# Gate and up of three feed-forward blocks by Strassen's scheme, four rounds of up and down, modulation dots on VectorE

## The reference, cut to what matters

```python
def swiglu(h, w1, w3, w2):
    return (jax.nn.silu(h @ w1) * (h @ w3)) @ w2

def _half_ffn(h, g, m, k, w1, w3, w2):
    y = swiglu(_modulate(h, g, m, k), w1, w3, w2)
    return h + (0.5 * m[:, :, 3 * k + 2] * y).astype(h.dtype)
```

## Time and profile before

| | |
|---|---|
| median of 3 runs | 2884.31 us (2883.98 to 2885.66) |
| span of the profiled execution (first to last instruction) | 2881.4 us |
| PE busy | 2789.6 us, 97% |
| DVE (VectorE) busy | 1520.7 us, 53% |
| ACT (ScalarE) busy | 1126.3 us, 39% |
| POOL (GpSimd) busy | 546.4 us, 19% |
| DMA | 258.76 MB, mean 90 GB/s |

### The profile page before, as it was taken

One profiled execution on the slowest core, in us unless ns is written; L12 is line 12 of the kernel. 1 busy time (PEld: TensorE's weight loads), 2 busy tenths in 40 slices (PEclk: granted clock), 3 DMA queues, 4 the chain that ended last, 5 costly groups with the idle time before them and its releaser, 6 DMA issues.

```text
span 2881.4 us, 40758 instructions
## 1 busy us (share of the span) xinstructions
PE 2789.6 (97%) x15696; PEld 2604.4 (90%) x15696; DVE 1520.7 (53%) x1919; ACT 1126.3 (39%) x1620; POOL 546.4 (19%) x264
## 2 busy tenths in 40 slices
PE   5999999999998999999999999999999999899999
PEld 5899999999986799999999999999998875788887
DVE  6974266564558668652664632222247657543332
ACT  3333134335547635331343422123324876532231
POOL 2442044210002522430442100000011520100000
PEclk8999999999999999999999999999999999999999
DMA  7443144212130014441442122212222110123232
GB/s 295 139 153 133 49 151 155 92 47 65 53 73 1 1 52 139 160 155 50 152 158 88 47 65 68 70 51 66 65 67 73 52 59 8 59 88 104 93 97 99
DMA packets 68391, 258.76 MB, mean 90 GB/s; under 512 B 7504, under 2 KB 9424, under 8 KB 67792
## 3 DMA queue, kind: packets, MB, share of 16 engines
q1 hardware_dynamic: 50736, 192.59, 20.3%
q10 hardware_dynamic: 17568, 65.02, 6.6%
HBM read 255.48 MB, written 2.10 MB: 89 GB/s over the span
## 4 chain that ended last, share of the span: by engine, by line
PE 86%; DVE 7%; issue 2%; ACT 2%; POOL 0%; DVEq 0%; POOLq 0%; ACTq 0%
PE banks L459 21%; PE banks L463 21%; PE banks L461 21%; PE banks L466 5%; PE banks L470 5%; PE banks L468 5%; DVE banks L1661 2%; PE banks L950 1%; PE banks L789 1%; DVE wl L1656 1%; PE banks L973 1%; DVE tmp L1849 1%; DVE xl L1841 1%; PE banks L873 1%; DVE nsS L2008 0%
## 5 line engine op out<-in xcount | busy, mean ns | idle before, releaser
L1079 ACT ACTIVATE wh<-raw 128x1024 fp32r<-128x1024 f32 (+1 forms) x300 | 338.8, 1129 | 1454.3 <-PE banks L463 1151.3
L459 PE MATMUL banks<-xh,wh 128*128 128x384 f32 x2608 | 671.6, 338 | 27.9 <-DVE wl L1656 15.8
L461 PE MATMUL banks<-xl,wh 128*128 128x384 f32 x2608 | 664.7, 335 | 0.0
L463 PE MATMUL banks<-xh,wl 128*128 128x384 f32 x2608 | 664.4, 335 | 0.0
L1656 DVE TENSOR_TENSOR wl<-raw,wh 128x1024 fp32r<-128x1024 f32 (+1 forms) x300 | 428.3, 1428 | 350.6 <-ACT wh L1079 349.8
L459 PEld LDWEIGHTS banks<-xh,wh 128*128 128x128 f32 x2608 | 471.7, 189 | 37.1 <-DVE wl L1656 19.0
L461 PEld LDWEIGHTS banks<-xl,wh 128*128 128x128 f32 x2608 | 473.9, 189 | 0.0
L463 PEld LDWEIGHTS banks<-xh,wl 128*128 128x128 f32 x2608 | 473.1, 189 | 0.0
L2419 POOL TENSOR_TENSOR mraw<-mraw,scb 128x1024 f32<-128x1024 f32 x120 | 316.1, 2635 | 636.2 <-DVE banks L1661 636.2
L463 PE MATMUL banks<-hh,wl 128*128 128x384 f32 x1056 | 267.9, 334 | 0.0
L461 PE MATMUL banks<-hl,wh 128*128 128x384 f32 x1056 | 267.9, 334 | 0.0
(11 more groups left out here) (368 smaller groups left out, 3240.4 us busy)
## 6 DMA issues: line engine op xcount, KB each, us to landing
raw<-in_w SPq DMA_DIRECT2D x176, 512.0 KB, 3.6
mraw<-in_wmn ACTq DMA_DIRECT2D x120, 512.0 KB, 4.4
raw<-in_w SPq DMA_DIRECT2D x64, 704.0 KB, 4.0
raw<-in_abin SPq DMA_DIRECT2D x24, 512.0 KB, 3.6
raw<-in_cdin SPq DMA_DIRECT2D x20, 512.0 KB, 3.6
mini<-in_wmn SPq DMA_DIRECT2D x9, 512.0 KB, 14.8
gmini<-in_wmn SPq DMA_DIRECT2D x2, 2048.0 KB, 21.8
raw<-in_about SPq DMA_DIRECT2D x8, 512.0 KB, 3.5
```

The source lines that it names most:

```text
L459: pe.matmul(bank(h), W, tokens(rh, h), start=(k == 0), stop=False)
L461: pe.matmul(bank(h), W, tokens(rl, h), start=False, stop=False)
L463: mm = pe.matmul(bank(h), L, tokens(rh, h), start=False, stop=(k == nk - 1))
L1079: act.activation(wh[slot][:, 0:nk * P], raw[slot][:, 0:nk * P], ACT.Copy).then_inc(hi_done, 1)
```

## The change

The gate and up products of ffn0, ffn1 and ffn2 are made in another way for chunks 4 to 21. Gate and up weights of a chunk, each cut in two at the middle of the 1024 inputs, are a 2x2 block matrix: A11, A12 (gate), A21, A22 (up). The activations are B11, B12 (inputs 0 to 511, even and odd blocks of tokens) and B21, B22. The Winograd form of Strassen's scheme is used:

- weight sums S1 = A21+A22, S2 = S1-A11, S4 = A12-S2 on VectorE (`weight_sum`), S3 = A11-A21 on GpSimd; each of S1, A11, S2, A22, S3, S4, A12 (128x512) is split in high and low part (`weight_hi` on ScalarE, `weight_lo` on VectorE);
- activation sums T1 = B12-B11, T2 = B22-T1, T3 = B22-B12, T4 = B21-T2, made once a block (`sums`, `sums_lo`, `first_sum_lo`) during its first group; T1 takes the place of B12 in `xh` and `xl`;
- seven products of 4 blocks x 3 matmuls x 384 columns in the order P1 = A11 B11, P5 = S1 T1, P6 = S2 T2, P7 = S3 T3, P3 = S4 B22, P2 = A12 B21, P4 = A22 T4;
- combinations u2 = P1+P6, uv = u2+P5, u2 = u2+P7, up's odd half = uv+P7, gate's odd half = uv+P3, up's even half = u2+P4 on VectorE, gate's even half = P2+P1 with a copy on ScalarE and the sum on GpSimd. Silu, the product and the split of the hidden chunk are then done by halves of 384 columns.

A block of ffn0 to ffn2 is now four rounds of up and down, of 4, 6, 6 and 6 chunks (the first with plain pairs), ffn3 three of 7, 7 and 8, all plain. The loops are written out. A modulation tile now gets both its dots on VectorE (`dot_mod`), none of the work on GpSimd or ScalarE. `mod_places` puts one tile beside each of the chunks 4 to 21, two beside chunks 2 and 3, and one beside each down tile of the second and third rounds (two beside two of them in ffn0, none beside two in ffn2), and 6 beside the last product of the ab mixer. The second half of the first gate's columns is loaded later, and its dots lie beside chunks 0 and 1. The other edits (semaphores that are merged, one transfer for the recurrence's weights) move nothing else.

```diff
-FH = FC // 2
+GROUPS = ((4, 6, 6, 6),) * 3 + ((7, 7, 8),)
+W_ORDER = ("S1", "A11", "S2", "A22", "S3", "S4", "A12")
+COMB_ORDER = ("U2", "U3", "C22", "C12", "C21")
...
+            def load_after_seven(t, s, src, nk):
+                slot = t % 2
+                sp.wait_ge(w_lo, w_count(s, "S3" if slot else "A12"))
                 sp.dma_start(raw[slot][:, 0:nk * P], src).then_inc(raw_landed[slot], 16)
...
+                            s = seven_pair(f, g, i)
+                            load_after_seven(t0 + 2 * i + 1, s - 1, src[1], KC)
+                            load_after_seven(t0 + 2 * i, s - 1, src[0], KC)
...
+            def seven_products(f, g, i):
+                pe.wait_ge(w_lo, w_count(s, "A11"))
+                pe.wait_ge(psum_free[1], t // 2 - 1)
+                product(P1_BANK[i % 2], "A11", *tokens(0, 0)).then_inc(p_done, 1)
+                pe.wait_ge(psum_free[0], t // 2)
+                product(P5_BANK, "S1", *tokens(0, 1)).then_inc(p_done, 1)
+                pe.wait_ge(w_lo, w_count(s, "S2"))
+                product(P6_BANK, "S2", *sums(0)).then_inc(p_done, 1)
+                if s:
+                    pe.wait_ge(comb_set, comb_count(s - 1, "C21"))
+                pe.wait_ge(w_lo, w_count(s, "S3"))
+                product(P7_BANK, "S3", *sums(1)).then_inc(p_done, 1)
+                pe.wait_ge(w_lo, w_count(s, "S4"))
+                pe.wait_ge(psum_free[1], t // 2)
+                product(P3_BANK, "S4", *tokens(4, 1)).then_inc(p_done, 1)
+                pe.wait_ge(w_lo, w_count(s, "A12"))
+                pe.wait_ge(half_set, 3 * s + 1)
+                product(P1_BANK[i % 2], "A12", *tokens(4, 0)).then_inc(mm_done, 1)
+                pe.wait_ge(comb_set, comb_count(s, "C22"))
+                product(P7_BANK, "A22", *sums(2)).then_inc(mm_done, 1)
...
+            def seven_act(f, g, i):
+                weight_hi(f, g, i, "A22")
+                weight_hi(f, g, i, "S3")
+                if i:
+                    hidden_hi(f, g, i - 1, 0)
+                act.wait_ge(p_done, 5 * s + 1)
+                act.activation(p1[:], P1_BANK[i % 2], ACT.Copy).then_inc(half_set, 1)
+                weight_hi(f, g, i, "S4")
+                weight_hi(f, g, i, "A12")
+                next_mods(f, ("up", first_chunk(f, g) + i))
+                if not last:
+                    weight_hi(f, g, i + 1, "S1")
+                act.wait_ge(comb_set, comb_count(s, "C12"))
+                act.activation(half(g1s[:], 1), half(g1s[:], 1), ACT.Silu).then_inc(half_set, 1)
...
+                    weight_hi(f, g, i + 1, "A11")
+                act.wait_ge(mm_done, t + 1)
+                act.activation(half(g1s[:], 0), thirds(P1_BANK[i % 2]), ACT.Copy).then_inc(psum_free[1], 1)
+                if not last:
+                    weight_hi(f, g, i + 1, "S2")
+                hidden_hi(f, g, i, 1)
+                act.wait_ge(pool_set, 2 * s + 2)
+                act.activation(half(g1s[:], 0), half(g1s[:], 0), ACT.Silu).then_inc(half_set, 1)
...
+            def last_quarter(f, g, i):
+                dve.wait_ge(mm_done, t + 2)
+                dve.tensor_tensor(half(hf[:], 0), thirds(u2), thirds(P7_BANK), ALU.add).then_inc(comb_set, 1)
+                dve.wait_ge(comb_set, comb_count(s, "C21"))
+                dve.wait_ge(half_set, 3 * s + 3)
+                dve.tensor_tensor(half(hf[:], 0), half(g1s[:], 0), half(hf[:], 0), ALU.mult).then_inc(hf_set, 1)
+
+            def seven_dve(f, g, i):
+                if i:
+                    last_quarter(f, g, i - 1)
+                weight_lo(f, g, i, "A22")
+                weight_lo(f, g, i, "S3")
+                if i:
+                    hidden_lo(f, g, i - 1, 0)
+                weight_lo(f, g, i, "S4")
+                dot_mods(f, ("up", first_chunk(f, g) + i))
+                if not last:
+                    weight_sum(f, g, i + 1, "S1")
+                dve.wait_ge(half_set, 3 * s + 1)
+                dve.wait_ge(p_done, 5 * s + 3)
+                dve.tensor_tensor(u2, p1[:], P6_BANK, ALU.add).then_inc(comb_set, 1)
+                dve.wait_ge(comb_set, comb_count(s, "U2"))
+                dve.tensor_tensor(uv, u2, P5_BANK, ALU.add).then_inc(psum_free[0], 1)
+                weight_lo(f, g, i, "A12")
+                if not last:
+                    weight_lo(f, g, i + 1, "S1")
+                dve.wait_ge(p_done, 5 * s + 4)
+                dve.tensor_tensor(u2, u2, P7_BANK, ALU.add).then_inc(comb_set, 1)
+                dve.wait_ge(psum_free[0], t // 2 + 1)
+                dve.tensor_tensor(half(hf[:], 1), thirds(uv), thirds(P7_BANK), ALU.add).then_inc(comb_set, 1)
+                dve.wait_ge(p_done, 5 * s + 5)
+                dve.tensor_tensor(half(g1s[:], 1), thirds(uv), thirds(P3_BANK), ALU.add).then_inc(comb_set, 1)
+                if last:
+                    split_lo(t + 2, 0, n)
+                else:
+                    weight_sum(f, g, i + 1, "S2")
+                    weight_lo(f, g, i + 1, "A11")
+                    weight_sum(f, g, i + 1, "S4")
+                dve.wait_ge(half_set, 3 * s + 2)
+                dve.wait_ge(comb_set, comb_count(s, "C22"))
+                dve.tensor_tensor(half(hf[:], 1), half(g1s[:], 1), half(hf[:], 1), ALU.mult).then_inc(hf_set, 1)
+                if not last:
+                    weight_lo(f, g, i + 1, "S2")
+                hidden_lo(f, g, i, 1)
...
-            def prod_mods(it0):
+            def seven_pool(f):
+                        for q in range(2):
+                            pool.wait_ge(raw_landed[q], 16 * (t // 2) + 16)
+                        if s:
+                            pool.wait_ge(w_lo, w_count(s - 1, "S3"))
+                        pool.tensor_tensor(W_SRC["S3"], W_SRC["A11"], W_SRC["A21"], ALU.subtract).then_inc(pool_set, 1)
+                        pool.wait_ge(psum_free[1], t // 2 + 1)
+                        pool.wait_ge(half_set, 3 * s + 1)
+                        pool.tensor_tensor(half(g1s[:], 0), half(g1s[:], 0), thirds(p1[:]), ALU.add).then_inc(pool_set, 1)
```

More of the change, by code:

```diff
@@ L65, with first_chunk, up_tile, down_tile @@
 N_TILES = _t
+def first_chunk(f, g):
+    return sum(GROUPS[f][:g])
+def up_tile(f, g):
+    return BASE[f"ffn{f}"] + 2 * first_chunk(f, g) + KC * g
+def down_tile(f, g):
+    return up_tile(f, g) + 2 * GROUPS[f][g]
+def seven(f, g):
+    return f < 3 and g > 0
+NSEVEN = FC - GROUPS[0][0]
+def seven_pair(f, g, i):
+    return NSEVEN * f + first_chunk(f, g) - GROUPS[f][0] + i
+_seven = [False] * N_TILES
+for _f in range(4):
+    for _g in range(len(GROUPS[_f])):
+        if seven(_f, _g):
+            for _q in range(2 * GROUPS[_f][_g]):
+                _seven[up_tile(_f, _g) + _q] = True
+PLAIN = [0]
+for _v in _seven:
+    PLAIN.append(PLAIN[-1] + (not _v))
+W_ORDER = ("S1", "A11", "S2", "A22", "S3", "S4", "A12")
+def w_count(s, name):
+    return 7 * s + W_ORDER.index(name) + 1
+COMB_ORDER = ("U2", "U3", "C22", "C12", "C21")
+def comb_count(s, name):
+    return 5 * s + COMB_ORDER.index(name) + 1
+def sum_count(s, name):
+    return 3 * s + ("S1", "S2", "S4").index(name) + 1
+def mod_places():
+    where = []
+    for f in range(3):
+        place = {}
+        for ch in (2, 3):
+            place["up", ch] = 2
+        for ch in range(4, FC):
+            place["up", ch] = 1
+        for g in (1, 2):
+            for j in range(KC):
+                place["down", g, j] = 1
+        if f == 0:
+            place["down", 1, 2] = place["down", 2, 2] = 2
+        if f == 2:
+            place["down", 2, 2] = place["down", 2, 5] = 0
+        where.append(place)
+    m, out = 0, []
+    for f in range(3):
+        start = m
+        table = {}
+        for g, n in enumerate(GROUPS[f]):
+            for key in [("up", first_chunk(f, g) + i) for i in range(n)] + [("down", g, j) for j in range(KC)]:
+                table[key] = range(m, m + where[f].get(key, 0))
+                m += where[f].get(key, 0)
+        out.append((start, m, table))
+        if f == 0:
+            m += AB_MODS
+    assert m == 120, m
+    return out
+W2_ROW = {}
+_rows = {}
+for _f in range(4):
+    for _g, _n in enumerate(GROUPS[_f]):
+        W2_ROW[_f, _g] = _rows.get(_n, 0)
+        _rows[_n] = W2_ROW[_f, _g] + 1
+AB_MODS = 6
+MODS = mod_places()
+AB_MOD0 = MODS[0][1]
 PCOL = {}
@@ new lines, in dot_mod, with dot_mods @@
+            def dot_mod(m, vec, vec_n, bufs):
+                dve.wait_ge(mod_landed[m % 2], 16 * (m // 2) + 16)
+                dve.wait_ge(scb_ready, vec_n + 1)
+                for q in range(2):
+                    if m + q:
+                        dve.wait_ge(mod_dot, 2 * m + q)
+                    dot(bufs[m % 2][:], q, vec, M[:, 24 + m, q:q + 1]).then_inc(mod_dot, 1)
+            def dot_mods(f, key):
+                for m in MODS[f][2][key]:
+                    dot_mod(m, scb, 1 if f == 0 else f + 2, mraw)
@@ L2513, in host_arrays @@
             w13.append(np.stack([t1, t3], 1).reshape(2 * FC, P, D))
[L2514 to L2516 removed]
```

(6 more changed lines are left out.)

732 lines of the change are left out of this document (449 added, 283 removed).

## The result

The kernel after takes 2974.34 us (median of 4, 2971.82 to 2980.07), the kernel before beside it 2884.14 (2882.34 to 2885.66): 1.0319 times as long, 95% interval 1.0304 to 1.0333. The forecast was 2941 with a range of 2855 to 2990, slower: right in sign and in the range, 33 us short. It lies 4 us above the range of the likeliest case alone, 2907 to 2970.

What follows compares the result with a forecast made beforehand. VectorE's list, with GpSimd's hold and load waits, was to bound chunks by seven at 17.95 us against TensorE's 14.55. Span 2881.4 + 61 - 8.3 + 4 = 2938, plus 2.9 for the runs' median: 2941 us, range 2855 to 2990.

Steps and rivals of the forecast that it cites:

- the likeliest case: VectorE's list as walked, with a round of 17.2 to 18.6 us: 2907 to 2970 us, slower; chance 0.57.
- The walked round: Middle chunk by seven, from A12's low part to the next: VectorE's list with holds and load waits, 17.95 us.
- hold: VectorE operations with two SBUF inputs stand still beside GpSimd's sums of 512 and 384 columns: 1.85 us a chunk.
- `raw[0]`: VectorE idle ahead of S2's sum until the load issued after A12's low part lands: 1.9 us a chunk.
- `raw[1]`: VectorE idle ahead of S1's sum until the load asked for after S3's low part lands: 0.3 us.
- The rival that GpSimd does not hold VectorE: GpSimd's two short sums cost VectorE nothing: round 16.0 us, 2855 us; half the hold, 2900; chance 0.17.
- The rival of later loads: Modulation loads overlap the load of `raw[0]`: 1.2 to 2.0 us more a chunk, 2970 to 3031 us; chance 0.12.
- The rival with TensorE as the bound: VectorE needs under 14.55 us a chunk, so TensorE sets the pace: 2777 us, up to 2850 with small stalls; chance 0.14.
- The group of six: Round of six chunks by seven: 11.0 head, 5 x 17.95, then 5.8, 106.6 us against 99.8; nine rounds, +61.
- (b): First group's down tiles: the first chunk by seven's weights come late, 1.3 us in three blocks, +4.
- (a): ffn0's first four chunks, relieved of the gate's dots as bound: from 74.80 to 66.5 us, -8.3.
- (c) to (f): Six-block down tiles, dots beside the ab output, removed GpSimd and ScalarE work with ffn3, written-out loops: all hidden or 0.

Runs made afterwards that it cites:

- the 16-column run: Kernel after the change with GpSimd's two sums of a chunk by seven cut to 16 columns: 2881.41 us, ratio 0.9998 to the kernel before.
- The run on the head: Version with reordered VectorE list and both GpSimd sums on VectorE, last down tile's modulation load issued after A22's and S3's high parts: 2826.94 us, ratio 0.9799.
- the mended order: Change with u2, uv, A12's low part before the dots, S1's sum between them, ScalarE's S1 and A11 high parts earlier, GpSimd's sums kept: 2845.45 us, ratio 0.9866.

## Why the prediction came out as it did

**The walked round: right.** 17.95 us were predicted; the 36 chunk intervals after the first of each round (by TensorE's first matmul of each chunk) have a mean of 17.84. Its parts: hold 1.85 predicted (1.05 and 0.8), 1.89 measured (1.08 and 0.81); `raw[0]` 1.9 predicted, 1.8 over all chunks and 2.1 in these 36; `raw[1]` 0.3 predicted, 0.24. But 17.84 is a mean of two kinds. 22 chunks have 17.4 on the mean, some 0.5 less than walked. The other 14 have 18.5, and there `raw[0]` lands 4.4 us after its issue instead of 3.7 and VectorE waits 2.6 us for it instead of 1.8. The chunk from 2008.90 to 2028.50 has the longest such wait; its row, and the row of the load (KB, us from issue to landing):

```profile
2027.19 0.69 DVE L2000 TENSOR_TENSOR ssum<-ssum,raw 128x512 f32<-128x512 f32 x1 [4.00 <-issue]
raw<-in_w SPq DMA_DIRECT2D x1, 512.0 KB, 5.9
```

The granted clock is not what makes them long: it is full in this chunk, and the four of the 36 that ran in part at the lower level (0.91 on the mean, one of them 201.90 to 220.50) have the same mean, 17.85, as the other 32. So the walk was too long by 0.5 us where the loads came as reckoned, and later loads gave 0.4 back on the mean; the two errors cancel, which the walk can't claim.

The rival that GpSimd does not hold VectorE falls with the 16-column run: the hold was worth the whole loss. Its size, 1.85, was right, but not the reason given for it, that the hold is shorter than GpSimd's instruction. In all of the 45 chunks VectorE's operation ends the same time after GpSimd's, 0.55 us for S4's sum and 0.42 for the multiplication, so it stands still until GpSimd is through. It is issued 0.19 and 0.51 us after GpSimd's, when 0.95 and 1.22 us of that are left. The earlier trace rows say the same: the dot is issued at 1202.77 and GpSimd's multiplication ends at 1205.11, 2.34 us later, where the hold is 2.21. Taken as a lock for the whole GpSimd instruction (the Trainium skill, SBUF — State Buffer, Who interferes with whom) it would have been 2.2 us. The trace agrees with such a lock, if the wait is counted from the moment at which VectorE's operation is issued: 0.95 + 1.22 = 2.17, each hold some 0.14 short of it.

The rival of later loads is true in part: it had 1.2 to 2.0 us in every chunk, and 14 of 36 chunks are 1.1 us longer than the rest, some 15 us in all. Why these loads land late is not shown; a modulation tile is under way beside `raw[0]` for about 1 us of its time in both kinds. The rival with TensorE as the bound is nearly what the change can be (14.93 against 14.55), but not in this order of work. Two of the rivals' sums are off: 11.0 + 5 x 14.55 + 5.8 is 89.6, which gives 2784 and not 2777, and a load that costs 54 us more gives 2995 and not 2970.

**The group of six: 107.6 on the mean against 106.6.** The head was right for the first round of a block (9.4) and too short for the other two: A12's low part ends 14.6 us after the round's begin on the mean of the six, where 11.8 was walked. The walk let ScalarE's copies run freely; in truth ScalarE stands in the written order behind a modulation load that waits for the dots:

```profile
1368.33 0.63 ACT L1336 ACTIVATE wh<-ssum 128x512 fp32r<-128x512 f32 x1 [4.66 <-DVE banks L1931]
1372.24 0.34 ACTq L1276 DMA_DIRECT2D mraw<-in_wmn  x1
1372.68 0.63 ACT L1336 ACTIVATE weh<-raw 128x512 fp32r<-128x512 f32 x1 [3.72 <-DVE banks L1931]
```

This cost six times 2.8 us, 17 in all, and what follows the head came out 0.8 us a round shorter than walked, 7 back: +70 for the nine rounds against +61. The run on the head shows that the place of this load is a part of it.

**(b), the first groups' down tiles: the step that was mis-sized**, +26 where +4 was forecast. It looked at one late weight tile at the end, 1.3 us a block, and took for granted that chunks 2 and 3 with their activation sums fit in their own time. They don't end there. The down stretch of ffn1 begins with chunk 3's sums:

```profile
1174.11 0.95 DVE L1973 TENSOR_TENSOR tmp<-xh,xl 128x768 f32<-128x768 f32 x1
...
1179.41 1.36 DVE L1983 TENSOR_TENSOR tl<-tf,th 128x1152 fp32r<-128x1152 f32 x1 [1.23 <-ACT th L1307]
...
1181.10 0.88 DVE L2115 SCALAR_TENSOR_TENSOR x<-banks,modG,x 128x256 f32<-128x256 f32 x2
...
1182.28 0.68 DVE L1926 TENSOR_TENSOR wl<-raw,wh 128x512 fp32r<-128x512 f32 x1
...
1183.02 1.01 PE L610 MATMUL banks<-hh,wh 128*128 128x384 f32 x2 [3.29 <-DVE wl L1926]
```

The first tile is evicted at 1181.10, and TensorE, which waits 3.29 us for the split behind it, goes on at 1183.02 at half the clock (0.32 us a matmul) for some 5 us. In the whole stretch VectorE has 36.39 us of work, where TensorE needs 33.3. The right question was the sum of VectorE's work over the stretch, not its last dependency.

**(a)** gave -12.8 over ffn0's first eleven chunks where -8.3 was forecast. The first four chunks take 70.74 us on TensorE where they took 79.13 before, which is the forecast -8.3 almost to the digit; the first of them is still 20.7 long and the other three 16.6 to 16.8. The other 4.4 came in chunks 5 and 6, which took 19.39 and 18.32 before. The forecast had looked at 79.66 to 154.46, which on TensorE holds chunks 2 to 5 and not the first four. **(c) to (f)**, forecast at nothing, came to 7 in all: 4 in the other down tiles, 3 in the plain chunks and the ab and cd inputs.

Sum of the misses: 9 us in the rounds, 22 in (b), 7 in small ones, less 4.5 in (a): 33.5 of the 34 us by which the forecast span of 2938 fell short of 2971.9.

Of the signs that were to show it, TensorE's busy share did not come: 84 to 89% in the rounds above, where 81% was forecast. Its matmuls are recorded longer than their distance, so that the share counts more than 84 x 0.1732 = 14.55 us of a chunk. VectorE is busy for 83 to 85% of these rounds, where over 85% was forecast.

## What to carry to other kernels

A scheme that trades matmuls for sums is priced by the other engines' list per chunk: write that list down, and with it the time from the last reader of a load buffer to the first reader of its next content, and put the independent work in between; here the order of a dozen lines was worth 129 us and made a 3% loss a 1.3% gain. Short GpSimd work is dear where VectorE has two operands in SBUF beside it; sums as short as these were better on VectorE in both orders (by 26 and by 11 us). On an engine that issues loads between its computations, look at what each such issue waits for, since the computations behind it wait too (3.72 us here ahead of A22's high part).

## What the runs showed of the hardware

The hold by GpSimd is mutual. Its sum of 512 columns takes 1.28 us at the shortest, where VectorE's operation beside it takes an operand from PSUM, and 1.74 on the mean of the 45 chunks in which it is issued while S4's sum, with two inputs in SBUF, is on VectorE for another 0.6 us. In the chunk shown the two engines take turns: GpSimd's sum of 384 columns ends at 1246.60, S4's sum at 1247.14, GpSimd's of 512 at 1248.29, the multiplication at 1248.70.

In the order of the change the hold costs its full length: 93 us for 54 chunks are 1.72 each, the sum of the two operations' excess. In the mended order the excess is 0.57 + 1.00 us a chunk (1264 - 690 and 1561 - 558 ns) and 0.14 more on the low parts of the sums (216 of them, 720 ns on the mean instead of 684), as much as before. VectorE's own sums would be 1.07, and the two versions differ by 0.3; in the one without GpSimd VectorE is idle for 0.6 us a chunk instead of 0.2, so it waits for something else by then and could not show all of the difference.

With two thirds of the matmuls left out TensorE was granted 0.53 of its clock in the round shown. In the kernel after, with TensorE idle for 2 to 3 us a chunk, 32 of the 36 chunks had the full clock and four a part at the lower level; what sets them apart was not found.
